# Inner layer norms of a two-layer trunk: totals as the moving operand, last tile added on GpSimd, mean subtracted before scaling

## The chip, the cores and the metric

One core of a Trainium2 chip runs the whole program. The metric is the device time of one execution in microseconds; lower is better. Times are given for three executions, and one further execution was taken with the profiler.

## The reference, cut to what matters

The program is a decoder trunk of two layers over 512 tokens of 1024 features, all in float32. Each layer mixes tokens, projects (`@ w_o`), adds the residual and normalises, then runs a squared-ReLU MLP of width 4096, adds the residual and normalises again:

```python
y = jnp.concatenate([mix, mo], axis=-1) @ w_o[layer]
x = layer_norm(DN_ALPHA * x + y, ln_g[layer, 0], ln_b[layer, 0])
x = layer_norm(DN_ALPHA * x + sq_relu_mlp(x, w_up[layer], w_down[layer]),
               ln_g[layer, 1], ln_b[layer, 1])
```

`layer_norm` takes mean and variance over the 1024 features of a token, and gives `(x - mu) * rsqrt(var + 1e-5) * g + b`. There are four such norms. The change concerns the first three; the last one is computed in another layout and is not touched.

## The kernel before

**Layout.** The residual stream `x32` lies turned: features on the 128 partitions, in eight tiles of features (k = 0 to 7), tokens along the free dimension. A norm's statistics are thus sums over partitions and over the eight tiles. Products are made in a split form: every operand is a high part (fp32r) and a low part (the rest), and a product is three matmuls, high by high, high by low, low by high. So each normed tile must be delivered as `x_hi` (ScalarE) and `x_lo` (GpSimd, `trunk_lo`, L2036), and each weight block as `w_hi` (ScalarE, `prepare`, L1105) and `w_lo` (VectorE, `prepare`, L1497). A weight block is called a unit. Units land by DMA from SP's queue in two alternating buffers `w_raw`; a load waits until VectorE has made the low part of the unit before it (L453), and units 28 to 31 are the first ones of the first MLP.

**The three norms.** n = 0 follows the output projection of layer 0 (`out_projection(0)`), n = 1 its MLP (`feed_forward(0)`), n = 2 the output projection of layer 1. Each norm is worked in two halves of 256 tokens (h = 0, 1), so that TensorE can compute the second half of the last projection blocks while the first half is normed. The names below carry both, as do the semaphores' counts.

**The sums.** VectorE adds the residual of tile j (`part_residual`, L1732), ScalarE squares the tile (`part_squares`, L1254), and GpSimd adds tile and square into `total` and `total_sq` (`add_tile`, L2081; `add_part`, L2093), for tiles 0 to 6. `layer_sums` (L849) then sums over partitions on TensorE in four steps: `total` and `total_sq` (128 partitions x 128 tokens at a time) are the stationary operand and a column of ones moves, which puts the sums of 128 tokens on 128 partitions, one column. Tile 7 and its square are added by further products of the same kind. The first two steps ("early") stand after the last block of the half, the other two ("late") three products-of-three later.

**The moments.** `moments` (L1755) on VectorE and `root` (L1265) on ScalarE work on columns of [128, 2]: mean, mean squared, variance, root, reciprocal (rstd), mean times rstd. `layer_spread` (L868) turns these columns back on TensorE: each column is broadcast and transposed against the identity, so that rstd and mean times rstd stand in PSUM on all partitions, for 256 tokens each.

**The finish.** `finish` on VectorE (L1771) multiplies each tile by the rstd in PSUM and subtracts the product of mean and rstd in PSUM ("move"); `finish` on ScalarE (L1270) applies gain and bias and makes `x_hi`; GpSimd makes `x_lo`.

**The order of the work** is written out by hand for each engine. What stands around the norms is this. On TensorE: in norms 0 and 2 the blocks 4 to 7 of the projection for the second half follow the first half's sums, in norm 1 blocks 6 and 7. Then, in norms 0 and 1, `memory_pair` (L1067): two projections of the memory of layer 1, of 24 products of 256 columns each, among which stand the second half's sums; then `project_two` (L761), the first two blocks of the next stage, which takes `x_hi` and `x_lo` tile by tile, first for half 0, then for half 1. In norm 2 there is no memory pair, and the second half's sums stand inside `project_two`. On ScalarE (out_projection, L1344): `finish` of the first half is interleaved with squares of the second half and with the high parts of two more units; after it stand the root of the second half, then `prepare(28)`, the memory keys, `prepare(29)`, the memory keys, `prepare(30)` and only then `finish(0, 1)` (L1441 to L1446). On VectorE (L1847): residuals of tiles 4 and 5 of the second half stand inside `finish` (behind k = 0 and k = 4), those of 6 and 7 behind it, each after the low part of a unit. On GpSimd (`layer_norm`, L2103): adds of the second half stand between the `x_lo` of the first.

## Time and profile before

| | us |
|---|---|
| median of 3 executions | 1173.56 (1173.42 to 1174.15) |
| profiled execution, device time | 1174.6 |
| its span in the trace | 1172.8 |
| TensorE busy | 1147.3 (98%) |
| VectorE busy | 622.7 (53%) |
| ScalarE busy | 489.2 (42%) |
| GpSimd busy | 134.8 (11%) |

PE is TensorE, PEld its weight loads, DVE is VectorE, ACT ScalarE, POOL GpSimd, SP the queue that issues most DMAs. A line of the trace names the kernel's line, the operation and the tiles, output before input. Durations of one instruction are its own; those that follow each other on an engine overlap by about a tenth of a microsecond, and matmuls by more, so that the distance from start to start tells the pace. In brackets stands the engine's idle time before an instruction and what ended it. The granted clock is that of TensorE, 1.00 being full speed.

### The profile page before, as it was taken

How to read it: one execution, taken by the hardware profiler on the slowest of the kernel's cores; microseconds unless marked ns; L12 is line 12 of the kernel's file. 1: busy time of each engine (PE TensorE's matmuls, PEld its weight loads, DVE VectorE, ACT ScalarE, POOL GpSimd, SP SyncE). 2: the span in 40 equal slices, each digit the busy share in tenths (PEclk: the TensorE clock that was granted, in tenths of full speed). 3: DMA queues.
4: the chain of work that ended last, by engine and by line, in shares of the span. 5: the costliest groups of instructions: out<-in, count | busy, mean ns of one | idle time of the engine just before them, and what ended most of it. 6: DMA issues, size and time to landing. Idle time of an engine off the chain costs nothing.

```text
span 1172.8 us, 16522 instructions
## 1 busy us (share of the span) xinstructions
PE 1147.3 (98%) x5860; PEld 969.4 (83%) x5860; DVE 622.7 (53%) x1069; ACT 489.2 (42%) x847; POOL 134.8 (11%) x156
## 2 busy tenths in 40 slices
PE   7999999999999999999999999999999999999997
PEld 7887899888888888889778888789888888888886
DVE  5668657444223444345588778856444223444226
ACT  5456347434122343224765565536434122333220
POOL 4300045000000000223300010045000000000000
PEclk9999999999999999999999999999999999999999
DMA  6522242233333333333211211133233333333332
GB/s 215 148 72 72 68 131 82 81 91 106 93 105 90 91 106 92 98 98 91 55 55 54 73 54 54 54 96 103 72 91 105 93 104 90 90 89 106 91 108 90
DMA packets 185591, 107.23 MB, mean 91 GB/s; under 512 B 4482, under 2 KB 180162, under 8 KB 185540
## 3 DMA queue, kind: packets, MB, share of 16 engines
q1 hardware_dynamic: 183236, 101.04, 30.1%
q10 hardware_dynamic: 2304, 5.51, 1.4%
q8 instruction: 33, 0.54, 0.2%
q14 instruction: 18, 0.15, 0.0%
HBM read 104.43 MB, written 2.10 MB: 91 GB/s over the span
## 4 chain that ended last, share of the span: by engine, by line
PE 86%; DVE 7%; ACT 4%; issue 1%; DMA 1%; ACTq 0%; DVEq 0%; SPq 0%
PE proj L537 70%; PE pv L537 3%; PE sc L537 2%; PE sc L896 2%; PE proj L896 2%; PE pv L896 2%; PE tr L896 2%; DVE w_lo L1495 2%; PE tr L588 2%; ACT w_hi L1111 1%; DMA mem_nat<-in_mem 1%; DVE sc L1557 1%; ACT x L1281 0%; DVE probs L1576 0%; DVE split_lo L1495 0%
## 5 line engine op out<-in xcount | busy, mean ns | idle before, releaser
L1495 DVE TENSOR_TENSOR w_lo<-w_raw,w_hi 128x1024 fp32r<-128x1024 f32 x171 | 217.9, 1274 | 166.9 <-ACT w_hi L1111 118.6
L537 PE MATMUL proj<-x_hi,w_hi 128*128 128x512 f32 (+1 forms) x768 | 298.9, 391 | 2.8 <-ACT x_hi L1283 1.3
L537 PE MATMUL proj<-x_hi,w_lo 128*128 128x512 f32 (+1 forms) x768 | 294.0, 384 | 0.0
L537 PE MATMUL proj<-x_lo,w_hi 128*128 128x512 f32 (+1 forms) x768 | 289.3, 384 | 0.0
L1111 ACT CAST w_hi<-w_raw 128x1024 fp32r<-128x1024 f32 x158 | 165.1, 1045 | 207.1 <-PE proj L537 200.1
L537 PEld LDWEIGHTS proj<-x_hi,w_hi 128*128 128x128 f32 x768 | 144.6, 188 | 31.4 <-ACT x_hi L1283 2.9
L537 PEld LDWEIGHTS proj<-x_hi,w_lo 128*128 128x128 f32 x768 | 144.6, 188 | 29.0
L537 PEld LDWEIGHTS proj<-x_lo,w_hi 128*128 128x128 f32 x768 | 142.5, 189 | 25.5
L537 PE MATMUL proj<-h_hi,w_hi 128*128 128x512 f32 (+1 forms) x384 | 146.3, 381 | 0.4 <-DVE w_lo L1495 0.4
L537 PE MATMUL proj<-h_hi,w_lo 128*128 128x512 f32 (+1 forms) x384 | 146.0, 380 | 0.0
L537 PE MATMUL proj<-h_lo,w_hi 128*128 128x512 f32 (+1 forms) x384 | 146.0, 380 | 0.0
L1798 DVE TENSOR_TENSOR h_raw<-relu 128x512 f32<-128x512 f32 x64 | 44.2, 691 | 158.7 <-ACT relu L1142 158.7
L1142 ACT ACTIVATE relu<-proj 128x512 f32<-128x512 f32 x64 | 38.2, 597 | 196.8 <-PE proj L537 196.8
L537 PEld LDWEIGHTS proj<-h_hi,w_hi 128*128 128x128 f32 x384 | 72.2, 188 | 14.4 <-DVE w_lo L1495 0.6
L537 PEld LDWEIGHTS proj<-h_hi,w_lo 128*128 128x128 f32 x384 | 72.2, 188 | 13.8
L537 PEld LDWEIGHTS proj<-h_lo,w_hi 128*128 128x128 f32 x384 | 72.2, 188 | 13.7
L2041 POOL TENSOR_TENSOR x_lo<-x,x_hi 128x256 fp32r<-128x256 f32 (+1 forms) x56 | 53.2, 963 | 48.0 <-ACT x L1279 25.6
L1711 DVE SCALAR_TENSOR_TENSOR x<-x,proj 128x512 f32 (+1 forms) x26 | 17.9, 687 | 66.6 <-PE proj L537 66.6
L1174 ACT ACTIVATE probs<-sc,neg_max 128x128 f32<-128x128 f32 (+2 forms) x64 | 33.0, 516 | 47.4 <-DVE neg_max L1557 35.7
L2091 POOL TENSOR_TENSOR total<-x 128x512 f32<-128x512 f32 x3 | 4.7, 1577 | 416.2 <-DVE x L1718 416.2
L1495 DVE TENSOR_TENSOR h_lo<-h_raw,h_hi 128x512 f32 (+1 forms) x64 | 44.3, 692 | 14.9 <-ACT h_hi L1295 14.4
L1295 ACT ACTIVATE h_hi<-relu 128x512 f32 (+1 forms) x64 | 40.5, 633 | 7.4
(358 smaller groups left out, 1784.5 us busy)
## 6 DMA issues: line engine op xcount, KB each, us to landing
w_raw<-in_w_up SPq DMA_DIRECT2D x64, 512.0 KB, 4.0
w_raw<-in_w_down SPq DMA_DIRECT2D x64, 512.0 KB, 3.9
w_raw<-in_w_o SPq DMA_DIRECT2D x16, 512.0 KB, 3.9
w_raw<-in_a_w_in SPq DMA_DIRECT2D x14, 512.0 KB, 3.8
w_raw<-in_kv_w SPq DMA_DIRECT2D x12, 512.0 KB, 3.8
w_raw<-in_mem_w_kv SPq DMA_DIRECT2D x8, 512.0 KB, 5.0
w_raw<-in_b_w_q SPq DMA_DIRECT2D x8, 512.0 KB, 4.0
x_nat<-in_x ACTq DMA_DIRECT2D x2, 1024.0 KB, 12.2
```

Source lines behind the costliest of these rows:

```text
L537: last = pe.matmul(target, lhs, rhs, start=start and n == 0, stop=stop and n == len(terms) - 1)
L588: last = pe.transpose(bank[0:n, at:at + rows], piece, ident[0:rows, 0:rows])
L896: last = pe.matmul(rows_of[t][n][:, :], lhs, rhs, start=False, stop=stop and m == 2, skip_group_check=True)
L1111: act.copy(weights(b)[0], w_raw[:, b.slot]).then_inc(w_hi_ready, 1)
L1142: act.activation(target, proj[g.slot][:, 0:target.shape[-1]], function).then_inc(proj_free[g.slot], 1)
L1174: act.activation(probs[:, u % 2, 0:n], sc[u % 2][:, 0:n], ACT.Exp, bias=neg_max[:, u:u + 1], scale=-1.0 if fox(s) else 1.0, accum_out=row_ ...
L1295: act.activation(h_hi[:, bass.ds(tile.at(), 1), :], relu[:, tile.slot:tile.slot + 1, :], ACT.Square).then_inc(h_hi_ready, 1)
L1495: return dve.tensor_tensor(target, whole, hi.bitcast(F32), ALU.subtract)
L1557: dve.tensor_tensor_reduce(own, own, causal[:, T - n:T], -1.0, -MASKED, ALU.add, ALU.min, neg_max[:, u:u + 1]).then_inc(max_done, 1)
L1711: dve.scalar_tensor_tensor(out=tile if target is None else target, in0=tile, scalar=ALPHA if first else 1.0, in1=proj[g.slot][:, :], op0=A ...
L1798: dve.tensor_tensor(raw, wide, wide, ALU.mult).then_inc(relu_sq, 1)
L2041: pool.tensor_tensor(x_lo[:, k, own], x32[:, k, own], x_hi[:, k, own].bitcast(F32), ALU.subtract).then_inc(x_ready, 1)
```

## The change

- `layer_sums` now takes ones [128, 128] as the stationary operand and lets `total` (q = 0) or `total_sq` (q = 1) move, 256 tokens in one f32 product. The sums come out on all 128 partitions of the bank, for all tokens. Nothing is turned back: `layer_spread` is gone.
- Tile 7 and its square are added into the totals by GpSimd, for both halves (for the second half before the `x_lo` of tile 4, in norm 1 of tile 6). TensorE's sums wait for these adds.
- The sum of values stands five products-of-three after the last block (before: early sums at once), the sum of squares two later. In `project_two` of norm 2 they stand behind (0, 6) and (1, 1).
- `moments` and `root` work on [128, 256] tiles; mean, variance and rstd lie in SBUF, in the places of `total`, `square` and `total_sq`.
- The finish subtracts the mean first (`centre`), two tiles ahead, the first two inside `moments` while the root is awaited; then it multiplies by rstd. Both now read their second operand from SBUF.

The diff, cut to its core (`feed_forward` is changed like `out_projection`; semaphores are renamed accordingly):

```diff
@@ -99,7 +99,7 @@
     EARLY_UNITS = LEAD_UNITS + [22, 118, 26, 27, 28, 29, 30, 31, 92, 93, 94, 122, 123, 124, 125]
-    PART0, SQ0, ADD0 = [0, 4, 6], [0, 12, 22], [0, 9, 16]
+    PART0, SQ0, ADD0 = [0, 4, 6], [0, 12, 22], [0, 11, 20]
     HT = T // 2
@@ -240,11 +240,6 @@
         square = put("square", [P, 2, T], F32, L0 + 8 * K1)
-        ln_mean = put("ln_mean", [P, TT], F32, L0 + 12 * K1)
-        ln_var = put("ln_var", [P, TT], F32, L0 + 12 * K1 + 64)
-        ln_sqrt = put("ln_sqrt", [P, TT], F32, L0 + 12 * K1 + 128)
-        ln_rstd = put("ln_rstd", [P, TT], F32, L0 + 12 * K1 + 192)
-        ln_move = put("ln_move", [P, TT], F32, L0 + 12 * K1 + 256)
         low = L0 + 12 * K1 + 512
@@ -367,7 +362,7 @@
-            return ADD0[n] + j + (0 if h is None else h * (KT - 1 - WHOLE[n]))
+            return ADD0[n] + j + (0 if h is None else h * (KT - WHOLE[n]))
@@ -832,12 +827,11 @@
                         memory_transposes(1, j - 2)
-                layer_sums(n, 0, True)
-                part(4, 1, (0, 3))
-                layer_sums(n, 0, False)
-                part(4, 1, (3, KT - 1))
-                layer_spread(n, 0)
-                part(4, 1, (KT - 1, KT))
+                part(4, 1, (0, 5))
+                layer_sums(n, 0, 0)
+                part(4, 1, (5, 7))
+                layer_sums(n, 0, 1)
+                part(4, 1, (7, KT))
                 for j in range(5, KT):
@@ -846,34 +840,12 @@
-            def layer_sums(n, h, early):
...
-                g = part_g(n, h, KT - 1)
-                for bank, adds, sums, done, count, last_tile in (
-                        (stat[h][0], sum_added, total, proj_free[g.slot], g.half(2), x32[:, KT - 1]),
-                        (stat[h][1], sq_added, total_sq, sq_ready, squared(n, KT - 1, h), square[:, 1])):
-                    if early:
-                        pe.wait_ge(adds, added(n, KT - 2, h))
-                    else:
-                        pe.wait_ge(done, count)
-                    part = (sums if early else last_tile)[:, tokens(h)]
-                    for t in range(TT // 2):
-                        last = pe.matmul(bank[:, t:t + 1], part[:, t * P:(t + 1) * P], ones_f[:, 0:1],
-                                         start=early and t == 0, stop=not early, skip_group_check=True)
-                    if not early:
-                        last.then_inc(stat_done, 1)
-            def layer_spread(n, h):
-                for q, column in enumerate((ln_rstd, ln_move)):
-                    pe.wait_ge(ln_step, 5 * (2 * n + h) + 4 + q)
-                    for t in range(TT // 2):
-                        one = column[:, 2 * h + t:2 * h + t + 1]
-                        last = pe.transpose(stat[h][q][:, t * P:(t + 1) * P], one.broadcast_to([P, P]), ident[:, :])
-                    last.then_inc(spread_done, 1)
+            def layer_sums(n, h, q):
+                adds, sums = ((sum_added, total), (sq_added, total_sq))[q]
+                pe.wait_ge(adds, added(n, KT - 1, h))
+                pe.matmul(stat[h][q][:, 0:HT], ones_r[:, :].bitcast(F32), sums[:, tokens(h)],
+                          start=True, stop=True).then_inc(stat_done, 1)
@@ -936,8 +908,7 @@
                     elif layer:
-                        project_two(b, g, 2, {(0, 1): lambda: layer_sums(2, 1, True), (0, 4): lambda: layer_sums(2, 1, False),
-                                              (1, 3): lambda: layer_spread(2, 1)})
+                        project_two(b, g, 2, {(0, 6): lambda: layer_sums(2, 1, 0), (1, 1): lambda: layer_sums(2, 1, 1)})
                     else:
@@ -1066,14 +1036,12 @@
-                memory_projection(1, first, (0, 2))
-                layer_sums(n, 1, True)
-                memory_projection(1, first, (2, 5))
-                layer_sums(n, 1, False)
-                memory_projection(1, first, (5, KT))
-                memory_projection(1, first + 1, (0, 1))
-                layer_spread(n, 1)
-                memory_projection(1, first + 1, (1, KT))
+                memory_projection(1, first, (0, 4))
+                layer_sums(n, 1, 0)
+                memory_projection(1, first, (4, 6))
+                layer_sums(n, 1, 1)
+                memory_projection(1, first, (6, KT))
+                memory_projection(1, first + 1)
             memory_pair(0, 0)
@@ -1263,15 +1231,15 @@
             def root(n, h):
-                own = slice(2 * h, 2 * h + 2)
-                act.wait_ge(ln_step, 5 * (2 * n + h) + 3)
-                act.activation(ln_sqrt[:, own], ln_var[:, own], ACT.Sqrt, bias=eps[:, 0:1]).then_inc(ln_root, 1)
+                own = tokens(h)
+                act.wait_ge(ln_step, 4 * (2 * n + h) + 3)
+                act.activation(total_sq[:, own], square[:, 0, own], ACT.Sqrt, bias=eps[:, 0:1]).then_inc(ln_root, 1)
...
                 for k in tiles:
-                    act.wait_ge(fin_moved, KT * m + k + 1)
+                    act.wait_ge(fin_scaled, KT * m + k + 1)
                     gain = dict(bias=par[:, 32 + KT * n + k:33 + KT * n + k], scale=par[:, KT * n + k:KT * n + k + 1])
@@ -1752,38 +1720,40 @@
+            def centre(n, h, k):
+                own = tokens(h)
+                dve.tensor_tensor(x32[:, k, own], x32[:, k, own], total[:, own], ALU.subtract).then_inc(fin_centred, 1)
...
-                m, own = 2 * n + h, slice(2 * h, 2 * h + 2)
+                m, own = 2 * n + h, tokens(h)
+                mean, var, rstd = total[:, own], square[:, 0, own], total_sq[:, own]
+                sum_bank, sq_bank = (bank[:, 0:HT] for bank in stat[h])
                 dve.wait_ge(stat_done, 2 * m + 1)
-                dve.tensor_scalar(ln_mean[:, own], stat[h][0][:, 0:2], 1.0 / D, None, ALU.mult).then_inc(ln_step, 1)
-                dve.wait_ge(ln_step, 5 * m + 1)
-                dve.tensor_tensor(ln_var[:, own], ln_mean[:, own], ln_mean[:, own], ALU.mult).then_inc(ln_step, 1)
-                dve.wait_ge(ln_step, 5 * m + 2)
+                dve.tensor_scalar(mean, sum_bank, 1.0 / D, None, ALU.mult).then_inc(ln_step, 1)
+                dve.wait_ge(ln_step, 4 * m + 1)
+                dve.tensor_tensor(var, mean, mean, ALU.mult).then_inc(ln_step, 1)
+                dve.wait_ge(ln_step, 4 * m + 2)
                 dve.wait_ge(stat_done, 2 * m + 2)
-                dve.scalar_tensor_tensor(out=ln_var[:, own], in0=stat[h][1][:, 0:2], scalar=1.0 / D, in1=ln_var[:, own],
+                dve.scalar_tensor_tensor(out=var, in0=sq_bank, scalar=1.0 / D, in1=var,
                                          op0=ALU.mult, op1=ALU.subtract).then_inc(ln_step, 1)
+                centre(n, h, 0)
+                centre(n, h, 1)
                 dve.wait_ge(ln_root, m + 1)
-                dve.reciprocal(ln_rstd[:, own], ln_sqrt[:, own]).then_inc(ln_step, 1)
-                dve.wait_ge(ln_step, 5 * m + 4)
-                dve.tensor_tensor(ln_move[:, own], ln_mean[:, own], ln_rstd[:, own], ALU.mult).then_inc(ln_step, 1)
+                dve.reciprocal(rstd, rstd).then_inc(ln_step, 1)
...
-                def move(k):
-                    dve.wait_ge(spread_done, 2 * m + 2)
-                    dve.wait_ge(fin_scaled, KT * m + k + 1)
-                    dve.tensor_tensor(x32[:, k, own], x32[:, k, own], stat[h][1][:, 0:HT], ALU.subtract).then_inc(fin_moved, 1)
-                dve.wait_ge(spread_done, 2 * m + 1)
+                dve.wait_ge(ln_step, 4 * m + 4)
                 for k in range(KT):
-                    dve.tensor_tensor(x32[:, k, own], x32[:, k, own], stat[h][0][:, 0:HT], ALU.mult).then_inc(fin_scaled, 1)
-                    if k != 1:
-                        move(max(k - 1, 0))
+                    dve.wait_ge(fin_centred, KT * m + k + 1)
+                    dve.tensor_tensor(x32[:, k, own], x32[:, k, own], total_sq[:, own], ALU.mult).then_inc(fin_scaled, 1)
+                    if k + 2 < KT:
+                        centre(n, h, k + 2)
                     for other in between.get(k, ()):
                         other()
-                move(KT - 1)
@@ -2105,13 +2075,15 @@
                     add_tile(n, Pos(j), Pos(g + j))
-                for j in range(WHOLE[n], KT - 1):
+                for j in range(WHOLE[n], KT):
                     add_part(n, j, 0)
...
                         add_part(n, KT - 2, 1)
+                    if k == (6 if n % 2 else 4):
+                        add_part(n, KT - 1, 1)
                     trunk_lo(2 * n + 1, k, tokens(0))
```

## Rows read from the trace of the kernel before

**Rows 1.** The page, busy us and share of the span of each engine, and instructions.

```profile
PE 1147.3 (98%) x5860; PEld 969.4 (83%) x5860; DVE 622.7 (53%) x1069; ACT 489.2 (42%) x847; POOL 134.8 (11%) x156
```

**Rows 2.** Waits of TensorE: us in total, times, longest.

```profile
PE tr L588 <- DVE probs L1571: 2.5, 2, 2.0
```

**Rows 3.** Timeline of TensorE, first half of the first norm (start us, us, what).

```profile
172.96 0.50 PE L863 MATMUL sc<-eps_one,total 128*128 128x1 f32 x4
...
173.78 0.36 PE L537 MATMUL proj<-mix_hi,w_hi 128*128 128x256 f32 x1
...
174.93 0.51 PE L863 MATMUL sc<-eps_one,x 128*128 128x1 f32 x4
...
175.74 0.36 PE L537 MATMUL proj<-mix_hi,w_hi 128*128 128x256 f32 x1
...
177.25 0.38 PE L875 MATMUL sc<-ident,ln_rstd 128*128 128x128 f32 x2
...
177.61 0.36 PE L537 MATMUL proj<-mix_hi,w_hi 128*128 128x256 f32 x1
```

**Rows 4.** Timeline of VectorE and ScalarE, the same half.

```profile
173.16 0.42 DVE L1744 SCALAR_TENSOR_TENSOR x<-x,proj 128x256 f32<-128x256 f32 x1 [1.43 <-PE proj L537]
...
178.65 0.60 ACT L1277 ACTIVATE x_hi<-x,par 128x256 fp32r<-128x256 f32 x1 [2.17 <-DVE x L1778]
...
178.87 0.74 DVE L1781 TENSOR_TENSOR x<-x,sc 128x256 f32<-128x256 f32 x2
...
181.36 0.42 DVE L1744 SCALAR_TENSOR_TENSOR x<-x,proj 128x256 f32<-128x256 f32 x1
```

**Rows 5.** Timeline of all engines, second half of the first norm.

```profile
187.88 0.50 PE L863 MATMUL pv<-eps_one,total 128*128 128x1 f32 x4
...
188.83 0.41 DVE L1744 SCALAR_TENSOR_TENSOR x<-x,proj 128x256 f32<-128x256 f32 x1
...
191.47 0.29 ACT L1268 ACTIVATE ln_sqrt<-ln_var,eps_one 128x2 f32<-128x2 f32 x1
...
194.12 0.37 SPq L454 DMA_DIRECT2D w_raw<-in_w_up  x1
...
198.31 1.05 ACT L1111 CAST w_hi<-w_raw 128x1024 fp32r<-128x1024 f32 x1 [1.32 <-DMA w_raw<-in_w_up]
```

**Rows 6.** GpSimd: adds by form (busy us, mean ns), and one x_lo on the timeline.

```profile
L2101 POOL TENSOR_TENSOR total<-total,x 128x256 f32<-128x256 f32 x14 | 10.3, 739 | 29.9 <-DVE x L1744 24.1 <-DVE x L1742 5.8
...
206.21 0.73 POOL L2041 TENSOR_TENSOR x_lo<-x,x_hi 128x256 fp32r<-128x256 f32 x1 [0.20 <-ACT x_hi L1283]
```

**Rows 7.** A PSUM subtraction by form; timeline of GpSimd and VectorE at 528 us.

```profile
L1778 DVE TENSOR_TENSOR x<-x,sc 128x256 f32<-128x256 f32 x24 | 9.7, 412 | 0.3
...
527.40 2.27 POOL L2091 TENSOR_TENSOR total_sq<-total_sq,square 128x512 f32<-128x512 f32 x1
...
528.45 1.77 DVE L1730 TENSOR_TENSOR x<-x,shift 128x512 f32<-128x512 f32 x1
...
531.28 0.68 DVE L1730 TENSOR_TENSOR x<-x,shift 128x512 f32<-128x512 f32 x1
```

**Rows 8.** Reciprocals by line: ns min/median/max, first and last start.

```profile
L1574 DVE RECIPROCAL inv_sum<-row_sum x64: 152/164/167, 45.1 to 758.3; 128x1 f32<-128x1 f32 x64
...
L1620 DVE RECIPROCAL sgu_rstd<-sgu_root x1: 167/167/167, 102.9 to 102.9; 128x4 f32<-128x4 f32 x1
```

**Rows 9.** Timeline, second half of the third norm.

```profile
811.53 0.38 PE L537 MATMUL proj<-x_hi,w_hi 128*128 128x256 f32 x1 [0.44 <-ACT x_hi L1283]
...
817.01 0.60 ACT L1281 ACTIVATE x<-x,par 128x256 f32<-128x256 f32 x1 [0.62 <-DVE x L1778]
```

**Rows 10.** Stretch of 5 us with mean granted clock; products on the timeline around it.

```profile
585.00:590.00 5.00, 3.09 (x14) 2.68 (x15) 2.95 (x10) 2.51 (x10) 0.00 (x0) 0.83 0.37 108
...
580.36 0.39 PE L537 MATMUL proj<-x_hi,w_hi 128*128 128x512 f32 x1
...
589.24 0.63 PE L537 MATMUL proj<-x_lo,w_hi 128*128 128x512 f32 x1
```

More of the change, by code:

```diff
@@ L319, in trunk_kernel @@
         sq_ready, sum_added, sq_added = sem("sq_ready"), sem("sum_added"), sem("sq_added")
-        stat_done, spread_done = sem("stat_done"), sem("spread_done")
+        stat_done = sem("stat_done")
         ln_step, ln_root = sem("ln_step"), sem("ln_root")
@@ L323, in trunk_kernel @@
         z_turned, z_out, z_gelu = sem("z_turned"), sem("z_out"), sem("z_gelu")
-        fin_scaled, fin_moved, fin_ready = sem("fin_scaled"), sem("fin_moved"), sem("fin_ready")
+        fin_centred, fin_scaled, fin_ready = sem("fin_centred"), sem("fin_scaled"), sem("fin_ready")
         y_counted, y_step, y_rooted = sem("y_counted"), sem("y_step"), sem("y_rooted")
@@ L975, in feed_forward @@
                                 part(j, 0, c)
-                        layer_sums(n, 0, True)
-                        part(6, 1, 0, (0, 3))
-                        layer_sums(n, 0, False)
-                        part(6, 1, 0, (3, KT - 1))
-                        layer_spread(n, 0)
-                        part(6, 1, 0, (KT - 1, KT))
+                        part(6, 1, 0, (0, 5))
+                        layer_sums(n, 0, 0)
+                        part(6, 1, 0, (5, 7))
+                        layer_sums(n, 0, 1)
+                        part(6, 1, 0, (7, KT))
                         part(6, 1, 1)
```

## The prediction

> **What bounds the kernel now.** First the page's busy time: TensorE works for 98% of the span, every other engine for little over half [rows 1]. Time is therefore won only by removing TensorE work, or lost by making TensorE wait. Then TensorE's waits: apart from the start, the longest is 2.0 us, behind a VectorE product in the attention [rows 2]; at the norms there are only small gaps. The changed code runs in six half norms (three norms, 256 tokens each), so I read the timeline of one of them and carried it to the others, which repeat it.
>
> In the first half of the first norm TensorE pays for the sums in three places [rows 3]: early sums 172.96 to 173.78 (0.82 us), late sums 174.93 to 175.74 (0.81), turned-back columns 177.25 to 177.61 (0.36). Between the first two, nine products of 256 columns take 1.15 us: 0.12 each and 0.08 more for the first after a break. So a half costs 1.99 us plus two to three breaks, about 2.2, or 13 us over six halves.
>
> **The new sums on TensorE.** Two f32 products with 256 moving columns replace this. No row shows one. Each old f32 product appears as two recorded pairs of load and product; if a pair passes the 256 columns once, a sum costs 2 x 0.12 = 0.24 us, if it passes them twice 0.48. The old pairs took 0.82/8 = 0.10 each for one column, so nothing excludes either end. I take 0.43, near the upper end, since the same pairs are issued and f32 data cannot be cheaper than the single passes beside it. The Trainium skill ("FP8 and Floating Point Precision", TensorE Precision Notes) says that true FP32 takes four passes; by it a sum would be 0.48 and the whole 0.6 us more, and no row here shows it. With two breaks a half costs 2 x (0.43 + 0.08) = 1.02 instead of 2.2: **-1.1 us a half, -6.6 us at most in all** (-8.8 and -6.4 at the ends).
>
> **First halves: hidden.** TensorE reaches the total 15 products (1.8 us) after the last block of the half, at 174.8. GpSimd now adds tile 7 behind the residual, which starts at 173.16 and lasts 0.42 [rows 4]: total at 173.6 to 174.35, squares to 175.1, with 0.74 for an add [rows 6]. Both are in time. The mean, its square and the variance grow from 2 to 256 columns, from some 0.16 (as the small reciprocals, [rows 8]) to 0.41 each (a 256-column VectorE operation, [rows 7]), the root from 0.29 [rows 5] to some 0.5; in exchange the turning back, the product of mean and rstd and one of two passes over tile 0 go. Square sums arrive at 176.7, variance 177.1, root 177.6, reciprocal 178.05, tile 0 scaled 178.5: the first x_hi starts at about 178.5 against 178.65 [rows 4]. Level.
>
> The **reciprocal** of 256 columns is not in the trace: 164 ns for one column, 167 for four [rows 8], so 1 ns a column and 0.41 us; from below it can't be under 0.16, from above I put 0.67 (2 ns a column).
>
> **Second halves: the gain goes into a wait.** TensorE is 1.1 us earlier, comes to the total at 187.5 in the first norm, and must find tile 7 in it. That tile's residual starts at 188.83 [rows 5], because VectorE makes a weight's low part before it, which waits for ScalarE, whose chain starts with x_hi; none of that moves earlier. The total is ready at 189.24 + 0.74 = 190.0. TensorE waits 2.4 us where it had work before, and ends the memory pair at the old time: -2.2 +2.4 = 0. Behind the waiting sum stand only TensorE's own products. The second norm does the same. In the third, the sum stands behind x_hi of tile 6, for which TensorE waits already (the next gap, 0.44 us, is tile 7's [rows 9]), so the gain is swallowed there as well.
>
> The root of that half comes later: square sums at 191.8, variance 192.25, root done 192.8, against a root at 191.47 + 0.29 [rows 5]: +1.0. Behind it on ScalarE's queue stands the high part of unit 28, then VectorE's low part, then SP's load of unit 30 (issued 194.12), whose landing releases ScalarE at 198.31 for unit 30 and only then for the second half's x_hi [rows 5]. TensorE runs on that x_hi chain to the end of the stage: +1.1 us in norm 1, about 0 in norm 2 (ScalarE there waits for the memory values), +0.2 in norm 3. **So far +1.3 us in place of -6.6.**
>
> **The shared port: the largest term.** All scalings and shifts of the finish read one operand from PSUM now: 0.412 us each, whatever GpSimd does [rows 7]. After the change both operands lie in SBUF. What that means is shown at 528 us: the subtraction of shift from x (two SBUF operands) takes 1.77 us when it meets GpSimd's sum, and 0.68 us three microseconds later when it doesn't; GpSimd's own add of 512 columns took 2.27, where twice the 0.74 for 256 columns [rows 6] makes 1.5, having been behind a VectorE operation [rows 7]. Each waited for the other's whole instruction, in the order in which they came. The Trainium skill ("SBUF — State Buffer", Who interferes with whom) gives this as an exclusive lock on the port pair that VectorE shares with GpSimd, taken by a VectorE instruction with two SBUF inputs; it speaks against this change, and the rows agree. By the rule all 96 finish operations fall under it; without it the sum stops at +1.3.
>
> Price: a GpSimd operation of 0.74 holds a waiting VectorE one for some 0.6. Between the first scaling and the residual of tile 5 VectorE has ten operations (0.33 apart: a pair takes 0.74 [rows 4]) and GpSimd four (two adds of tile 4, two x_lo). That is 10 x 0.33 + 4 x 0.6 = 5.7 us after 178.1, so 183.8, against 181.36 now, where TensorE set it [rows 4]: +2.4. ScalarE's square of tile 5, the next weight's high and low parts, the residual of tile 6 and at last that of tile 7 hang on it in a row, so total and root of the second half move by 2.3 too. Norms 1 and 3: +2.3 each. Norm 2 has only tiles 6 and 7 to finish and fewer adds: +1.0. In the second half the mean's square and a centring meet x_lo once each: +0.4 per norm. In norm 3 x_hi of the second half has no lead over GpSimd (ScalarE waited 0.62 for the finish of tile 2 already [rows 9]), and from tile 3 a tile costs one x_lo and more than one held operation: 1.2 us in place of 0.93 [rows 6] for five tiles, +1.3, and 0.5 for the weight's low part in between. In norm 1 the load of unit 30 gives VectorE that lead: 0. Sum: norm 1 1.1 + 2.3 + 0.4 = 3.8; norm 2 0 + 1.0 + 0.4 = 1.4; norm 3 0.2 + 2.3 + 0.4 + 1.8 = 4.7. **+9.9 us.**
>
> **The clock.** After TensorE's wait of 2.0 us at 585 the granted clock averages 0.83 over five microseconds, and a product of 512 columns takes 0.63 us instead of 0.39 [rows 10]; seven such come in a row, 7 x 0.24 = 1.7 us. The new waits are as long: in norm 1 TensorE waits 2.2 us for the low part of the memory weight (2.3 later now, with 0.1 of slack after TensorE's gain) and again for total, in norm 2 for either, in norm 3 for x_hi of tile 6, each 2 to 3 us. Bounds 0 and 4 x 1.7 = 7; I take 2.0, as TensorE isn't always on the path behind them. Total +11.9.
>
> The profiled execution took 1174.6 us (span 1172.8 plus 1.8 around it), 1.0 above the median of 1173.56. 1174.6 + 11.9 = 1186.5 in that execution's terms; against the median **1185.5**.
>
> **The rivals.**
> A, faster, 1167.0, chance 0.12: the place is the last tile's add on GpSimd. If the residual of tile 7 came before 187.1, so that total is there at 187.9 when the old early sums stood there [rows 5], TensorE would keep its 1.1 us a half: 1173.56 - 6.6. For it: TensorE is 98% busy. Against: the residual starts at 188.83 and its chain is ScalarE's. It decides once the residual is 1.7 us earlier.
> B, no change, 1174.9, chance 0.12: VectorE's operations seldom meet GpSimd's, because they slip between; then only the +1.3 is left. For it: in the second half of norm 1 VectorE is ahead of the first x_lo. Against: in a finish GpSimd reads for 0.73 us of every 0.93 [rows 6].
> C, much slower, 1196, chance 0.07: the reciprocal takes 2.3 us, held 1.8 us longer in each half with everything behind it, 6 x 1.8 = +10.8. The Trainium skill ("VectorE: DVE Perf Modes", in its explanation of the eight slices) says that a reciprocal's divide steps run with a repeat count of 8; were that per element, this would be its time. The rows speak against it: three more columns cost 3 ns, not 25 [rows 8].
> D, the forecast, 0.69, own range 1179 to 1192: down with sums of 0.24 (-1.6), no clock term (-2) and half of the meetings missed (-3); up with sums of 0.48, a reciprocal of 0.67 (+1.4 together) and the clock term at 7 (+5). That the edit doesn't take effect isn't possible: tiles and engines are named in it.
>
> **How the numbers follow.** A measurement of this kernel tells 0.2% (2.3 us) from nothing. Faster: A, 0.12. Same: B, 0.12. Slower: C and D, 0.76. The range 1174 to 1192 holds B and D and leaves out A and C, 0.19.
>
> **What would show it.** Sums of 0.4 to 0.5 us on TensorE; reciprocal near 0.41; the finish's subtractions and products at a mean well over 0.41 (0.6 to 0.7) though alone they take 0.41; the residual of tile 7 some 2 us later after the last full block; TensorE waiting for GpSimd's total by 2 us or more in norms 1 and 2. If the finish operations stay at 0.41, the port term is wrong; if there is no TensorE wait for total, the second-half step is; if all norm stages are shorter than before, A holds.

## The result and the profile after

The changed kernel takes **1193.93 us** (median of 4 executions, 1192.35 to 1194.94) against 1173.61 for the kernel before, measured beside it (1173.42 to 1174.15): ratio 1.0171, 95% interval 1.0154 to 1.0189, 20.3 us slower. The forecast was slower, 1185.5, with a range up to 1192. Norms 1 to 3 are counted as in the prediction: norm 1 is n = 0 in the code. The profiled execution took 1193.62 us, its span is 1191.6 (before: 1172.8).

The page's busy time and the row of TensorE's granted clock in 40 slices, kernel after:

```profile
PE 1148.6 (96%) x5764; PEld 968.2 (81%) x5764; DVE 646.6 (54%) x1063; ACT 491.0 (41%) x847; POOL 149.2 (13%) x168
...
PEclk9999998999999999999999999998899999999999
```

TensorE has 96 instructions fewer than in [rows 1], yet is busy for 1.3 us longer: in one slice at norm 1 and two at norm 3 the granted clock is lower. VectorE is busy for 24 us more, GpSimd for 14.

The groups of instructions that changed (line, engine, operation, tiles, shapes, count; busy us, mean ns; idle before):

```profile
L1744 DVE RECIPROCAL total_sq<-total_sq 128x256 f32<-128x256 f32 x6 | 10.5, 1746 | 0.0
...
L1752 DVE TENSOR_TENSOR x<-x,total_sq 128x256 f32<-128x256 f32 x48 | 27.8, 589 | 0.2
...
L1726 DVE TENSOR_TENSOR x<-x,total 128x256 f32<-128x256 f32 x48 | 24.4, 518 | 0.0
...
L2011 POOL TENSOR_TENSOR x_lo<-x,x_hi 128x256 fp32r<-128x256 f32 (+1 forms) x56 | 59.5, 1087 | 45.4 <-ACT x L1247 28.0 <-ACT x_hi L1357 15.0 <-ACT x_hi L1251 2.2
```

The first row is the surprise: a reciprocal of 256 columns takes 1746 ns, where I had put 410. The next two answer to the PSUM subtraction in [rows 7]: 0.52 and 0.59 us on the mean instead of 0.412. x_lo, the last row, rose too: the 48 of 256 columns take 0.98 us on the mean, where they took 0.83 in the kernel before.

The waits of TensorE (us in total, times, longest), kernel after; [rows 2] had a single one of 2 us:

```profile
PE proj L532 <- DVE w_lo L1463: 7.7, 6, 4.3
...
PE proj L532 <- DVE x L1712: 5.6, 5, 2.0
PE proj L532 <- ACT x_hi L1251: 4.2, 4, 2.4
PE tr L583 <- DVE probs L1539: 2.6, 2, 2.0
PE pv L847 <- POOL total L2071: 2.0, 1, 2.0
```

The fourth was there before. The others stand at the norms: the low part of the memory weight (4.3 in norm 2), the residual that clears a PSUM bank, x_hi, and GpSimd's total. In the kernel before the longest wait for a low part was 0.7 us, for a residual 0.4, for x_hi 0.9, and none was for the total.

Now norm 1 as in [rows 3 to 5]. Its first half on the timeline (start us, us), kernel after: TensorE's sum of the values and what follows it, VectorE, two adds of GpSimd, and the first x_hi on ScalarE.

```profile
173.74 0.60 PE L847 MATMUL sc<-total,ones_r 128*128 128x256 f32 x2
...
173.98 0.47 PE L532 MATMUL proj<-mix_hi,w_hi 128*128 128x256 f32 x1
174.29 0.28 PE L532 MATMUL proj<-mix_lo,w_hi 128*128 128x256 f32 x1
174.41 0.28 PE L532 MATMUL proj<-mix_hi,w_lo 128*128 128x256 f32 x1
174.52 0.28 PE L532 MATMUL proj<-mix_hi,w_hi 128*128 128x256 f32 x1
...
176.59 1.75 DVE L1744 RECIPROCAL total_sq<-total_sq 128x256 f32<-128x256 f32 x1
178.37 0.43 DVE L1752 TENSOR_TENSOR x<-x,total_sq 128x256 f32<-128x256 f32 x1
...
179.71 0.96 DVE L1726 TENSOR_TENSOR x<-x,total 128x256 f32<-128x256 f32 x1
180.60 0.96 DVE L1752 TENSOR_TENSOR x<-x,total_sq 128x256 f32<-128x256 f32 x1
...
184.24 0.41 DVE L1712 SCALAR_TENSOR_TENSOR x<-x,proj 128x256 f32<-128x256 f32 x1
...
179.54 0.85 POOL L2071 TENSOR_TENSOR total<-total,x 128x256 f32<-128x256 f32 x1 [5.49 <-DVE x L1712]
180.45 0.83 POOL L2071 TENSOR_TENSOR total_sq<-total_sq,square 128x256 f32<-128x256 f32 x1
...
178.83 0.60 ACT L1245 ACTIVATE x_hi<-x,par 128x256 fp32r<-128x256 f32 x1 [2.28 <-DVE x L1752]
```

From the sum at 173.74 to the fourth product behind it (174.52) pass 0.78 us, and three products of 0.12 leave 0.42 for a sum with its breaks. While GpSimd is silent a finish operation takes 0.42; when it adds, 0.96, and GpSimd's own adds take 0.85 and 0.83 instead of 0.74 [rows 6]. The residual of tile 5 stands at 184.24, against 181.36 in [rows 4].

The second half, kernel after, TensorE and ScalarE:

```profile
193.07 1.22 PE L847 MATMUL pv<-total,ones_r 128*128 128x256 f32 x2 [2.04 <-POOL total L2071]
193.73 0.78 PE L532 MATMUL proj<-memt_hi,w_hi 128*128 128x256 f32 x1
194.30 0.41 PE L532 MATMUL proj<-memt_lo,w_hi 128*128 128x256 f32 x1
...
195.37 1.05 PE L847 MATMUL pv<-total_sq,ones_r 128*128 128x256 f32 x2
...
196.99 0.51 ACT L1236 ACTIVATE total_sq<-square,eps_one 128x256 f32<-128x256 f32 x1 [2.59 <-DVE square L1739]
...
204.58 1.06 ACT L1079 CAST w_hi<-w_raw 128x1024 fp32r<-128x1024 f32 x1 [1.92 <-DMA w_raw<-in_w_up]
```

TensorE waits 2.04 us for GpSimd's total, and behind that wait its products start 0.21 us apart instead of 0.12. The granted clock is 0.50 from 193 to 196 us, the level of 1.2 GHz instead of 2.4. Root and unit 30 come 5.5 and 6.3 us later than in [rows 5].

### The profile page after: what moved, and what is told of

Read it like the earlier page. It is cut to its first block, busy times and chain, and to the rows that moved or that the text cites. A ratio compares the mean times of both kernels' runs of the same rounds, so it can differ in the third digit from the quotient of the medians.

```text
span 1191.6 us, 16306 instructions
## 1 busy us (share of the span) xinstructions
PE 1148.6 (96%) x5764; PEld 968.2 (81%) x5764; DVE 646.6 (54%) x1063; ACT 491.0 (41%) x847; POOL 149.2 (13%) x168
## 4 chain that ended last, share of the span: by engine, by line
PE 79%; DVE 9%; ACT 4%; issue 3%; DMA 3%; POOL 2%; DVEq 0%; ACTq 0%; SPq 0%; POOLq 0%
PE proj L532 63%; PE pv L532 3%; PE sc L532 2%; PE proj L868 2%; PE pv L868 2%; PE tr L868 2%; PE sc L868 2%; DVE w_lo L1463 2%; PE tr L583 2%; POOL x_lo L2011 1%; DMA w_raw<-in_mem_w_kv 1%; ACT w_hi L1079 1%; DVE x L1752 1%; DVE x L1726 1%; DMA w_raw<-in_w_o 1%
## 5 line engine op out<-in xcount | busy, mean ns | idle before, releaser
L532 PEld LDWEIGHTS proj<-h_lo,w_hi 128*128 128x128 f32 x384 | 72.2, 188 | 13.9
L2011 POOL TENSOR_TENSOR x_lo<-x,x_hi 128x256 fp32r<-128x256 f32 (+1 forms) x56 | 59.5, 1087 | 45.4 <-ACT x L1247 28.0
```

Source lines behind the costliest of these rows:

```text
L532: last = pe.matmul(target, lhs, rhs, start=start and n == 0, stop=stop and n == len(terms) - 1)
L2011: pool.tensor_tensor(x_lo[:, k, own], x32[:, k, own], x_hi[:, k, own].bitcast(F32), ALU.subtract).then_inc(x_ready, 1)
```

## The experiments

Twelve kernels were run. Each stands beside executions of the kernel before on the same chip; "over before" is the difference of medians, and the interval is that of the ratio. One distance serves as a probe of the mechanism: in norm 1, from the residual of tile 7 of the first half to that of the second (before: 173.16 to 188.83 [rows 4, 5], 15.7 us).

| kernel | median us | over before | ratio, 95% interval | clock of the profile | probe us |
|---|---|---|---|---|---|
| after | 1193.93 | +20.3 | 1.0154 to 1.0189 | 0.989 | 19.5 |
| after, reciprocal left out | 1186.13 | +12.2 | 1.0088 to 1.0119 | 0.995 | 18.1 |
| after, operands in PSUM | 1183.98 | +10.1 | 1.0069 to 1.0096 | 0.994 | 16.9 |
| after, both | 1175.55 | +1.7 | 1.0008 to 1.0026 | 0.995 | 15.5 |

**1. The reciprocal left out.**

```diff
-                dve.reciprocal(rstd, rstd).then_inc(ln_step, 1)
+                dve.tensor_scalar(rstd, rstd, 0.0, 0.7, ALU.mult, ALU.add).then_inc(ln_step, 1)
```

> The changed kernel with the 256-column reciprocal replaced by a multiply-add of the same shape; it leaves out the reciprocal (every rstd is 0.7). Theory R (the reciprocal's 1.75 us, of which 1.34 is more than I had forecast, sits on the chain root, scaling, x_hi, next load in every half): the operation that stands in takes 0.41 us, and the time falls by 1.34 in each of six halves, slightly less where it is hidden: 6 to 8 us, to 1186 to 1188. Theory S (the surplus over the forecast comes from the clock and the sums, the reciprocal is hidden behind what VectorE could do meanwhile): under 2 us, 1192 to 1194.

Measured: 1186.13 us, 7.8 less than after (8.1 by the differences to before). Theory R. The operation that stands in took less than the 0.41 us expected:

```profile
176.53 0.28 DVE L1744 TENSOR_SCALAR total_sq<-total_sq 128x256 f32<-128x256 f32 x1
```

So 1.46 us are gone in each half, 8.8 in six, and nearly all of it shows. In the first half of norm 1 it all does: the probe is 1.47 us shorter. This is close to the kernel of my forecast, in which the operation takes 0.41: 1186.1 against 1185.5.

**2. The port term removed.**

```diff
-                dve.tensor_tensor(x32[:, k, own], x32[:, k, own], total[:, own], ALU.subtract).then_inc(fin_centred, 1)
+                dve.scalar_tensor_tensor(out=x32[:, k, own], in0=stat[h][0][:, 0:HT], scalar=-1.0 / D, in1=x32[:, k, own],
+                                         op0=ALU.mult, op1=ALU.add).then_inc(fin_centred, 1)
...
-                mean, var, rstd = total[:, own], square[:, 0, own], total_sq[:, own]
+                mean, var, rstd = total[:, own], square[:, 0, own], stat[h][1][:, HT:T]
```

(the scaling reads rstd from `stat[h][1]` as well)

> The changed kernel with the sums, their place and the reciprocal as they are, but no VectorE operation of the finish with two operands in SBUF: the centring takes the sum straight from its PSUM bank ((sum x -1/D) + x), and rstd is written to PSUM and read there by the scaling. Theory P (the two-SBUF finish operations exclude GpSimd's and wait for them): both operations stay at 0.41 us all through, GpSimd's x_lo falls back to 0.96 on the mean, and 7 to 9 us go: 1185 to 1187. Theory S (it is the number of operations and their order that costs, not where the operand lies): means of 0.52 and 0.59 stay or TensorE's waits stay, less than 2 us: 1192 or more.

Measured: 1183.98 us, 10.0 less than after. Theory P, and rather more than expected. The groups of this kernel:

```profile
L1726 DVE SCALAR_TENSOR_TENSOR x<-sc,x 128x256 f32<-128x256 f32 x24 | 9.7, 414 | 0.0
...
L1753 DVE TENSOR_TENSOR x<-x,sc 128x256 f32<-128x256 f32 x24 | 9.6, 410 | 0.1
...
L2012 POOL TENSOR_TENSOR x_lo<-x,x_hi 128x256 fp32r<-128x256 f32 (+1 forms) x56 | 53.4, 972 | 44.9 <-ACT x L1247 26.4 <-ACT x_hi L1357 15.4 <-ACT x_hi L1251 2.4
```

The same 96 operations with one operand moved to PSUM are back at 0.41 us. x_lo is back at 0.97, and its 48 operations of 256 columns at 0.84. By the rule on the shared port in the Trainium skill ("SBUF — State Buffer", Who interferes with whom) it is the second SBUF operand that takes the lock; this pair of runs agrees, at 10 us.

**3. Both.** The two edits together; the operation that stands in for the reciprocal writes to PSUM.

> Both edits in one: no two-SBUF operation in the finish, and the reciprocal left out (rstd is 0.7 throughout). If the two terms add, 1193.9 - 8 - 7 = 1179, and with what the clock gives back (1 to 2 us, as the waits of 2 us go) 1176 to 1179; by the sum of the forecast, with only its +1.3 for the order of the second halves left, 1174.9. If a third thing of 5 us or more costs time (the wait for GpSimd's total, the clock by itself), it stays at 1181 or more.

Measured: 1175.55 us, 1.7 over before. The terms add: 10.2 and 10.5 us for the port (with and without the reciprocal), 8.1 and 8.4 for the reciprocal (with and without the port). In this kernel the operation that stands in takes 0.42 us, 1.33 less than the reciprocal, so 8.0 of the 8.4 are its own time. What is left, 1.7, is what I had as "+1.3". The same square stands in the probe, for norm 1 alone: 19.5, 18.1, 16.9 and 15.5, so 2.5 to 2.7 for the port and 1.3 to 1.5 for the reciprocal. The page of this kernel, and its wait in norm 1:

```profile
PE 1142.7 (97%) x5764; PEld 963.5 (82%) x5764; DVE 625.9 (53%) x1063; ACT 490.1 (42%) x847; POOL 143.1 (12%) x168
```

```profile
PE pv L847 <- POOL total L2072: 2.2, 1, 2.2
```

TensorE works 4.6 us less than in [rows 1] and the kernel is still not faster: in norm 1 the gain goes into the wait of 2.2 us for GpSimd's total. Norm 2 has a second such wait, of 2.3. This also answers whether the wide form, in this order of the work, could win with a cheaper reciprocal or another port: even without both costs it is 1.7 us behind.

**4. The delay alone, in the kernel before.**

```diff
+                for c in range(2):
+                    dve.reciprocal(probs[:, 1, c * P:(c + 1) * P], ones_r[:, :].bitcast(F32)).then_inc(cop, 1)
                 dve.reciprocal(ln_rstd[:, own], ln_sqrt[:, own]).then_inc(ln_step, 1)
```

> The kernel before with two reciprocals of 128 columns (into a buffer nobody reads) ahead of its own reciprocal of two columns, in each of the six halves: some 1.6 to 1.9 us of VectorE's time at the place where the changed kernel spends 1.75, and nothing else changed. Theory R: what VectorE is late by at that place goes to the end of the stage, though TensorE's turned-back columns wait there too: 1.0 to 1.6 us a half, +6 to +10, 1180 to 1183. Rival: in the kernel before, TensorE's and ScalarE's own work covers it, under +2, 1175 or less; then the reciprocal hurts only where the port has already used up that cover.

Measured: 1181.26 us, +7.4 (interval 1.0045 to 1.0072). Theory R. In norm 1 the dummies hold the own reciprocal back by 1.7 us (176.34 to 178.02), six times that is 10, and 0.7 of it comes out at the end.

**5. What a reciprocal costs by its width.** Nine of them in a row at VectorE's start.

> The kernel before with nine reciprocals, one after another, at VectorE's start, of 1, 4, 8, 16, 32, 64, 128, 256 and 512 columns, into a buffer nobody reads yet; only their durations count. If a reciprocal costs a fixed part and 6.2 ns a column (1746 ns at 256 in the changed kernel), then about 160, 170, 200, 250, 350, 550, 940, 1740, 3330 ns. If the small ones of 161 and 168 ns hide a part that is flat up to some width, the first three or four are the same and the slope starts later; my reading of 1 ns a column from 1 and 4 columns would then have been no slope at all.

Timeline of VectorE in this kernel (start us, us):

```profile
1.52 0.16 DVE L1879 RECIPROCAL probs<-probs 128x1 f32<-128x1 f32 x1
1.72 0.18 DVE L1881 RECIPROCAL probs<-probs 128x4 f32<-128x4 f32 x1
...
2.46 0.35 DVE L1887 RECIPROCAL probs<-probs 128x32 f32<-128x32 f32 x1
...
4.42 1.75 DVE L1893 RECIPROCAL probs<-probs 128x256 f32<-128x256 f32 x1
6.21 3.35 DVE L1895 RECIPROCAL probs<-probs 128x512 f32<-128x512 f32 x1
```

A straight line from four columns on, and within 5 ns of it at one: 3.35 - 1.75 = 1.60 us for 256 columns more, 6.25 ns each, on some 0.15 us. From one to four columns that is 19 ns; here it is 14 (164 and 178 ns). In [rows 8] the medians differ by 3 ns, but the 64 reciprocals of one column alone spread from 152 to 167 ns. A slope can't be read from a difference smaller than that spread.

**6 and 7. The port alone, in the kernel before.** The control copies rstd and shift from PSUM to SBUF and doesn't use the copies; the second kernel uses them.

```diff
+                dve.wait_ge(spread_done, 2 * m + 2)
+                dve.tensor_scalar(total_sq[:, own], stat[h][0][:, 0:HT], 1.0, None, ALU.mult).then_inc(cop, 1)
+                dve.tensor_scalar(total[:, own], stat[h][1][:, 0:HT], 1.0, None, ALU.mult).then_inc(cop, 1)
...
-                    dve.tensor_tensor(x32[:, k, own], x32[:, k, own], stat[h][0][:, 0:HT], ALU.mult).then_inc(fin_scaled, 1)
+                    dve.tensor_tensor(x32[:, k, own], x32[:, k, own], total_sq[:, own], ALU.mult).then_inc(fin_scaled, 1)
```

(the last pair of lines, and the same for the shift, in the second kernel only)

> The kernel before with two extra VectorE copies in each half, rstd and shift from their PSUM banks into SBUF, which nobody reads: the finish still takes both from PSUM. The control of the next run. Two operations of 0.41 us ahead of the finish: 6 x 0.8 = up to +5 if all of it shows, as the 1.8 us of dummy reciprocals showed as 1.2 us a half; by that share (0.67) +3.3, about 1177. Under +1 would say that small delays there are covered.

> The same kernel, but now the finish reads the copies in SBUF: 96 VectorE operations with two SBUF operands where before they had one in PSUM, and nothing else of the change (old sums, old turning back, narrow reciprocal). Theory P (exclusion of VectorE's two-SBUF operations and GpSimd's): 7 to 11 us more than the control, 1184 to 1188, the finish operations at a mean of 0.52 to 0.59 instead of 0.41. Rival (the port costs only together with the later second halves of the new order): under 4 us more than the control, 1181 or less.

Measured: control 1179.65 us, +5.4 (1.0029 to 1.0057), above what I expected: all of the copies' 4.9 shows, and the first scaling now waits for both turned columns. With the copies in use 1201.62 us, +27.4 (1.0225 to 1.0253), so **22 us** for where the operands lie. That the port costs by itself is shown; the size missed the expectation of 7 to 11 by a factor of two. Groups and page of the second kernel:

```profile
L1778 DVE TENSOR_TENSOR x<-x,total 128x256 f32<-128x256 f32 x48 | 29.2, 619 | 0.6
L1784 DVE TENSOR_TENSOR x<-x,total_sq 128x256 f32<-128x256 f32 x48 | 29.0, 614 | 0.2
```

```profile
PE 1162.1 (97%) x5860; PEld 983.9 (82%) x5860; DVE 644.6 (54%) x1081; ACT 490.5 (41%) x847; POOL 138.3 (12%) x156
```

Beyond 0.41 us apiece the 96 operations take 20 us here, against 14 after the change (means of 0.59 and 0.52). And TensorE is busy for 13 us more than in the control (1148.9), with the same work: the granted clock is 0.983 instead of 0.996. The traces part the 22 us roughly. The three first halves, from residual of tile 7 to residual of tile 7, are 3.0, 1.8 and 3.0 us longer than in the control, 7.8 in all. Most of the rest lies in and behind the second halves. In norm 2 TensorE waits 3.0 us for the weight's low part and then works at a granted clock of 0.50 from 565 to 573. The residual of tile 7 comes meanwhile, and the mean starts 4.2 us behind it, against 1.1 in the control. So at that place the slower TensorE stands in the chain.

**8. The order of the finish.** The changed kernel with "mean first" undone: one more product, then scaling before subtracting.

```diff
-                centre(n, h, 0)
-                centre(n, h, 1)
...
                 dve.reciprocal(rstd, rstd).then_inc(ln_step, 1)
+                dve.wait_ge(ln_step, 5 * m + 4)
+                dve.tensor_tensor(mean, mean, rstd, ALU.mult).then_inc(ln_step, 1)
```

> The changed kernel with one part of the change undone: the mean is not taken off first; as in the kernel before, rstd x mean is formed after the reciprocal (one more 256-column operation), tiles are scaled and then shifted, all operands in SBUF. Theory M (taking the mean off first hides two centrings behind the root and saves the product, and otherwise both orders meet GpSimd alike): 0.41 us for the product and 0.34 for tile 0's shift later in each half, 6 x 0.75 x about 0.8 = +3 to +5, 1197 to 1199. Rival N (scaling and shifting from SBUF in the old order costs 22 us in the old kernel against the 10 us that the new order pays for the port, so the order itself carries much of that): +8 us or more, 1202 or more. Rival O (the order is worth nothing where the reciprocal leads): within 1.5 us of 1193.9.

Measured: 1201.43 us, 7.5 more than after, between M (3 to 5) and N (8 and more), nearer to N. The two expectations don't part cleanly, but the sign is plain: of all parts of the change, taking the mean off first is the one that wins, and more than the 0.75 us a half of VectorE time that it saves (4.5). In the trace the subtractions rise from 0.52 to 0.58 us on the mean, so they meet GpSimd more often. And while the root is awaited VectorE is now idle for 0.58 us a half, where it had centred two tiles. So the old order accounts for a part of the 22 us in the old kernel. What TensorE's clock adds there was not tried by itself.

**9 and 10. The last tile on GpSimd alone.** The kernel before with narrow sums and narrow reciprocal, but tile 7 added by GpSimd and one set of sums; first for both halves, then for first halves only.

```diff
-                    if early:
-                        pe.wait_ge(adds, added(n, KT - 2, h))
-                    else:
-                        pe.wait_ge(done, count)
+                if early:
+                    return
+                for bank, adds, sums in ((stat[h][0], sum_added, total), (stat[h][1], sq_added, total_sq)):
+                    pe.wait_ge(adds, added(n, KT - 1, h))
```

> The kernel before with the last tile added by GpSimd, one set of narrow sums (four pairs) at the late place in each half, all else as before. TensorE work falls by 0.82 + 0.08 a half, 5.4 us. Theory W (in the second halves the gain goes into the wait for GpSimd's total, and the square sums come later): 1173 to 1177, with a TensorE wait for total of 1 us or more in norms 1 and 2. Rival (the order is what keeps it: only the changed kernel's earlier place makes it wait): TensorE keeps the gain, 1168 to 1171.

> The same, in the first halves alone: there the adds are in time, the second halves keep two sets of sums. TensorE work falls by 0.9 us in three halves. Theory W: the first half is bound by TensorE, so 1 to 2.7 us are won, 1171 to 1172.6. Rival (what TensorE gains in a first half it gives back at the low part of the next weight, whose chain starts with x_hi and not with TensorE): within 1 us of the kernel before.

Measured: both halves 1177.37 us (11 executions, 1174.91 to 1178.6), +3.1, interval 1.0014 to 1.0032: Theory W, 0.4 above its upper end. The waits name it:

```profile
PE pv L859 <- POOL total L2096: 3.6, 3, 1.7
```

These waits take up the 3.1 us that TensorE works less (1144.2). The profile is of the fastest of the executions, 1174.9; what the others lose beyond it, no trace shows.

First halves alone: 1173.21 us against 1174.26, ratio 0.9993, interval 0.9984 to 1.0002. That is the rival: three times 0.9 us of TensorE work were to go (2.2 us by the page), and the medians differ by 1.0, which the interval doesn't part from nothing. It is the best version that I ran, and no measurable win.

**11. The sums of the second halves placed later.** From kernel 2, total's behind six tiles of the memory block instead of four, the squares' behind eight instead of six.

```diff
-                memory_projection(1, first, (0, 4))
+                memory_projection(1, first, (0, 6))
                 layer_sums(n, 1, 0)
-                memory_projection(1, first, (4, 6))
+                memory_projection(1, first, (6, KT))
                 layer_sums(n, 1, 1)
```

> The changed kernel with its port term removed (centring and scaling with an operand in PSUM), and the sums of the second halves of norms 1 and 2 moved back by two product groups: total's after the sixth tile of the memory block, the squares' after the eighth. Theory W (the wait for GpSimd's total only takes the gain up, its place does not matter since the chain behind it is ScalarE's and VectorE's): within 1.5 us of the same kernel with the sums at their place (1184.0). Rival (TensorE's wait of 2.2 us there is on the path by itself or through the clock): 2 us or more are won, 1182 or less; if the later square sums hold the root back instead, up to 1.5 slower.

Measured: 1183.34 us against 1183.98, within 1.5: Theory W. By the differences to before it is 1.0 less (9.1 and 10.1), which is not clear of the noise. In the traces the second half's x_hi comes 0.6 us sooner behind the residual of tile 7 in norm 1 and 0.5 in norm 2. So the place is worth about 1 us at most.

**12. The clock.** Idle products inside TensorE's five longest new waits.

```diff
+            def fill(moving, times):
+                for _ in range(times):
+                    pe.matmul(stat[1][0][:, 0:HT], ones_r[:, :], moving, start=True, stop=True)
```

> The changed kernel with idle products (256 columns, into a bank nobody reads, full speed 0.12 us each) where TensorE waits longest: 12 ahead of the residual of tile 6 in norms 1 and 3, 14 ahead of the second-half total in norm 1, 32 ahead of the memory block in norm 2, 16 ahead of x_hi of tile 6 in norm 3. All lie inside waits that were measured as 1.96, 2.04, 4.25, 1.98 and 2.42 us. Theory K (clock term of the forecast, +2.0, most of the half-speed time is hidden behind the chain of VectorE and ScalarE): granted clock up from 0.989 to 0.994 or more, time down by 1 to 3 us, 1191 to 1193. Rival K7 (the clock is the missing 7 us and more): 1187 or less. Rival K0 (no product there is on the path, or the filling only costs): 1193 to 1196.

Measured: 1193.59 us (1192.37 to 1193.88), interval 1.0149 to 1.0177: the time of after. The page of this kernel, granted clock 0.995:

```profile
PEclk9999999999999999999999999999999999999999
```

Most of the clock came back and the time didn't: of six stretches at half clock around the norms, 23 us in all, three of about 3 us each are left. Soon after each filling TensorE still waits for 0.6 to 1.4 us, so the idle products fit into the waits. By the medians this is rival K0. By the differences to before it is 1.0 us less than after (19.4 against 20.3), so that theory K's lower end of 1 us is not ruled out.

In norm 1 the slow products did stand before the root. It comes 3.8 us after the residual of tile 7 (196.17 less 192.35), against 5.3 in after (196.99 less 191.67). But x_hi starts 13.5 us after that residual (205.87), against 13.9 (205.54): of the 1.5 us 0.35 are left. VectorE's timeline shows where 1.0 of them went, first this kernel, then after:

```profile
196.05 1.78 DVE L1738 TENSOR_TENSOR x<-x,total 128x256 f32<-128x256 f32 x2
197.76 1.74 DVE L1756 RECIPROCAL total_sq<-total_sq 128x256 f32<-128x256 f32 x1
...
196.87 0.75 DVE L1726 TENSOR_TENSOR x<-x,total 128x256 f32<-128x256 f32 x2
197.54 1.75 DVE L1744 RECIPROCAL total_sq<-total_sq 128x256 f32<-128x256 f32 x1
```

The two centrings come early enough to run into GpSimd's x_lo (194.36 to 197.55) and take 1.78 us instead of 0.75. The reciprocal follows them, then the low part of unit 28, and on that the load of unit 30 depends. So what the clock gives back here, the port takes. The filling was not tried in a kernel without the port term.

## Why the prediction was wrong

- **TensorE work.** Predicted 0.43 and 0.08 for a break, 0.51 in all; measured 0.42 with the breaks. By that the work removed is 2.2 - 0.84 a half, about 8 us instead of 6.6; this is an estimate (the page of kernel 3 shows 4.6 us less busy time, part of it at half clock). The prediction's own terms, 2.2 - 1.02, make 7.1 and not 6.6, with ends of 9.4 and 6.5; the time it gave doesn't hang on this. Right in kind; and as predicted it buys nothing. The estimate of 0.48 from the four passes of the Trainium skill ("FP8 and Floating Point Precision", TensorE Precision Notes) is above what is seen here.
- **First halves: "level". This is the step that failed**, at the reciprocal: taken at 0.41 us, bounded at 0.67, measured 1.75. From the residual of tile 7 to the first x_hi pass 6.7 us (172.13 to 178.83) where 5.5 did [rows 4], and the 1.2 us more are that term. Without the reciprocal (kernel 1) it is 5.2 us, so the rest of this step held. Kernels 1 and 3 show that the term comes out at the end, at 8.1 to 8.4 us, and kernel 4 that a delay of 1.7 us at this place costs 7.4 by itself. The sum without it came out at 1186.1, 1185.5 predicted, but in part by luck: the port was 1.9 us dearer than its term and the clock 1 to 2 cheaper.
- **Second halves: the gain goes into the wait for the total.** Right: 2.04 us waited where 2.4 was predicted, in norm 1; in norm 2 it went into the wait for the memory weight instead (4.3), in norm 3 into x_hi. The +1.3 for this step measured 1.7 (kernel 3), and that is luck too. In the trace of kernel 3 the second half's x_hi comes 2.0, 1.6 and 1.2 us later behind the residual of tile 7 than in the kernel before, where the prediction had 1.1, 0 and 0.2; other stretches, 0.5 of them in the first halves, give back the difference. After the change, in norm 1, the root came 5.3 us after the residual instead of 3.5, as the sums ran at the lower clock.
- **The port.** Predicted 8.6 of the 9.9 us (the +1.3 is the step above); measured 10.2 and 10.5. In the first half of norm 1 the probe gave 2.5 to 2.7, predicted 2.3. The mechanism and nearly the size were right.
- **The clock.** Predicted 2.0, bounds 0 and 7; after the change six stretches run at half clock, but kernel 12 puts the cost at 0.3 by the medians and 1.0 by the differences to before, both within the noise. That is near the lower bound; in norm 1 the port takes what a faster clock gives. 1.7 + 10.3 + 8.3 + 0 = 20.3.
- **The rivals.** A and B didn't happen. C, the reciprocal that is paid for every column, is what happened, at 1.75 us instead of 2.3 and with 1193.9 instead of 1196; it had a chance of 0.07. The sentence of the Trainium skill ("VectorE: DVE Perf Modes", in its explanation of the eight slices) pointed the right way: divide steps that repeat. The runs show the price by the column; that the divide steps are its reason, no run shows. The rows were set against it, and these rows could not bear that, because their scatter (15 ns) was nearly as large as the effect (19 ns for three columns at 6.25). With 1.75 in the sum the forecast would have been 1185.5 + 8 = 1193.5.

## What to carry to other kernels

A small operation's time says nothing about its slope: before one is widened from a few columns to hundreds, price it by a row of some width, and if there is none, let the range reach to what a per-element cost would give. The narrow [128, 2] statistics, turned back on TensorE, looked wasteful, and were what kept an expensive reciprocal and a second SBUF operand out of a chain that sets the end. Where TensorE is 98% busy and still waits on a chain of VectorE and ScalarE at a stage's end, removing its work wins nothing there; moving VectorE operations in front of a wait, with one operation fewer (mean first, 7.5 us, measured inside the changed kernel), does.

## What the runs showed that was not expected

- VectorE's reciprocal: 6.25 ns a column of f32, linear from 1 to 512 columns, on about 0.15 us. A multiply of 256 columns takes 0.41, a reciprocal 1.75.
- The same 96 operations of the finish: 22 us for SBUF instead of PSUM operands in the old kernel, 10 in the new.
- An f32 product of 256 moving columns against stationary ones takes 0.42 us with its breaks, 3.5 times the 0.12 of an fp32r one.
- Half clock on TensorE that costs nothing measurable: with three of six such stretches left the clock is up from 0.989 to 0.995, the time 1193.59 instead of 1193.93. In norm 1 the products came sooner, and VectorE's centrings then met GpSimd's x_lo.
- `tensor_scalar` of 256 columns from SBUF to SBUF takes 0.28 us on VectorE (kernel 1), from SBUF to PSUM 0.42 (kernel 3).
